# The second block's output projection from F32 matmuls to high and low parts, with the splitting put into the tail of the mixer

## Chip, cores and metric

One core of a Trainium2 chip runs the whole kernel. The metric is the device time of one execution in microseconds, the median over runs. The kernel before takes 2604.84 us, median of three runs (2599.87 to 2604.89). The profiled execution is another one.

Names of the engines: PE is TensorE, PEld its weight loads, DVE is VectorE, ACT is ScalarE, SP issues the DMAs of the weights, POOL those of the modulation rows.

## The reference, cut to what matters

The program chains two transformer stacks over 256 latent tokens (and, in the second stack, 256 context tokens), model width 1024. The change is in the last layer of the second stack, layer 1, where only the latent tokens go on:

```
q, k, v = split(h @ w_in)                      # 16 heads of 64, 4 key/value heads
o_lat   = window_gqa(q, k, v, ...)             # softmax(q k + window mask, with sink) v
o_lat   = o_lat @ w_out                        # [256, 1024] @ [1024, 1024]   <- the change
x       = x + m_lat[5] * o_lat
x       = x + 0.5 * m_lat[8] * swiglu(modulate(rms_norm(x), ...), ffn_in, ffn_out)
return rms_norm(x, final_gain)
```

Everything is float32. A product `x @ w` is made in this kernel in one of two ways. Either as it stands, a matmul of type F32. Or on parts: `hi` is the operand rounded by a copy to the type fp32r (float32 "round"), `lo` is the operand less `hi`, also as fp32r, and the product is `w_hi x_hi + w_hi x_lo + w_lo x_hi`, three matmuls of type fp32r into the same bank of PSUM.

## The kernel before

The activations lie feature-major, `[128 partitions, 8 chunks (KC), tokens]`. Five engines run programs of their own, in order, and wait for each other by semaphores. The function `schedule` names the stages; each engine supplies its own version of each stage, and `barrier` between stages lets no engine go on before PE, ACT and DVE have drained.

Weights come as tiles of 1 MB (1024 rows by 256 columns, `TILE`) in the order of `weight_order`, into a ring of three slots (`RING`). SP asks for tile n once tile n-3 has been released (`tile_used`). A tile has two halves (m = 0, 1) of 128 output features.

PSUM has eight banks. All engines take them in the same order (`turns`); PE takes the bank after next only when the user of eight turns ago has freed it (`take_bank`, `bank_free`).

**The mixer of layer 1**, `blend(1)`, with `blend_order(1)`: the values, then ten halves of q and k (`half` 0 to 9), each a product on parts of 24 fp32r matmuls of 512 columns. For each half ACT copies the high part of the weights (`split_high`, line 1795) and DVE subtracts the low part (`split_low`, line 2306). Behind each half comes a `rope` step (PE line 1139, DVE lines 2444 to 2447). Beside them runs the attention, 16 pairs of units, chunk `j` of the output `ph4["o"]` made by pairs 2j and 2j+1. The steps, called "pair" i, are software-pipelined (`attention_pairs`), and within step i the engines do, each in this order:

- PE: the scores of pair i (line 1198), the outputs of pair i-3 (line 1214), the transposes of pair i-2 (line 1226)
- ACT: evicts the outputs of pair i-3 into `o` (line 1907), copies the two transposed p of pair i-2 to `pT` (line 1912), two exps of pair i (line 1918)
- DVE: for both units of pair i adds the mask and takes the maximum (lines 2511, 2512), then rescales pair i-1 (lines 2518, 2523)

Halves and steps interleave as half 9, rope 8, steps 10 and 11, rope 9, then steps 12 to 18 with no half left. Steps 16 to 18 have no scores any more. This stretch from step 10 on is called the tail of the mixer below. Then follow the barrier and the projection.

**The projection of layer 1**, `project("w_out_2o", 1, SEQ)`: 8 output chunks, for each 8 F32 matmuls (line 983) of 256 columns, read from the ring tile. The profile shows two records of each F32 matmul. Between tiles PE waits until the last product of the tile is complete (`take_tile`, line 901). For each chunk DVE adds the gated product to x (`gated_add`, line 2417), ACT squares it (line 1783), and PE sums the squares for the coming norm with F32 matmuls (`sum_squares`, line 938), two chunks at a time, in between.

**The projection of layer 0**, `project_parts`, is on parts already: it splits at its start the eight chunks of `o` and two weight halves, and one further half per chunk (lines 992, 1666, 2373). It follows the recurrence, and runs 512 tokens.

Of the kernel before, what the change touches and what calls it, by code (L numbers as in the profile page):

```python
# [32 lines left out]
P = 128  # L33
# [156 lines left out]
def schedule(s):  # L190
# [16 lines left out]
    s["project_parts"](TOK)  # L207
# [11 lines left out]
    s["project"]("w_out_2o", 1, SEQ)  # L219
# [74 lines left out]

def blend_order(layer):
# [11 lines left out]
    for at, item in enumerate(main + [("none", 0)]):  # L307
        yield item
        for what, later in places:
            for i, begun in enumerate(evicted):  # L310
                if begun + later == at:
                    yield what, i
        for i, place in enumerate(pairs):
            if place == at:
                yield "pair", i
        if layer == 0 and at == 19:
            yield "lora", 0

# [8 lines left out]
def weight_order():  # L327
# [7 lines left out]
    def project(name, layer, tok):  # L335
        for j in range(4):
            order.append((name, 0, j))

    def project_parts(tok):
        for j in range(4):  # L340
            order.append(("w_out_2e", 0, j))
# [24 lines left out]
    schedule(dict(blend=blend, project=project, project_parts=project_parts, mixer=mixer, leave=leave, ffn=ffn, **{n: quiet for n in names}))  # L366
# [39 lines left out]
def out_halves(order):  # L406

    at = order.index(("w_out_2e", 0, 0))
    return [Half("out", at + c // 2, c % 2, 0, KC, c) for c in range(KC)]
# [25 lines left out]
def build(nc, ins, out):  # L435
    order = weight_order()
    with ExitStack() as ctx:
# [70 lines left out]
        with ExitStack() as stack:  # L508
# [10 lines left out]
            for ph in (ph2, ph3):  # L519
# [4 lines left out]
                            "x_hi": parts_of_x, "x_lo": parts_of_x, "w_hi": parts_of_w, "w_lo": parts_of_w})  # L524
# [8 lines left out]
        parts_out = out_halves(order)  # L533
# [16 lines left out]


# [327 lines left out]
        def _(pe):  # L879
# [89 lines left out]
            def project(name, layer, tok):  # L969
                o = ph4["o"] if layer else ph2["o"]  # L970
                for c in range(KC):
                    m = c % 2
                    if m == 0:
                        w = take_tile()
                    bank, full = take_bank()
                    product = turns.n - 1
                    if m == 1 and c > 1:
                        sum_squares(c - 3, tok)
                        sum_squares(c - 2, tok)
                    for kc in range(KC):  # L980
                        if c == KC - 1 and kc == KC - 2:
                            sum_squares(KC - 2, tok)
                        mm = pe.matmul(bank[:, 0:tok], w[:, kc * COLS + m * P:kc * COLS + (m + 1) * P],  # L983
                                       o[:, kc, 0:tok], start=kc == 0, stop=kc == KC - 1)
                        if kc == 0:
                            first(mm)
                    mm.then_inc(full, 1)
                    if m == 1:
                        release_tile(product)
                sum_squares(KC - 1, tok)  # L990

            def project_parts(tok):

                b_w, b_o = tally("w_split", KC), tally("o_split", KC)
                for c, h in enumerate(parts_out):
# [5 lines left out]
                    high, low = mixed_half(0)(c)  # L1001
# [3 lines left out]
                    for kc in range(KC):  # L1005
# [4 lines left out]
                        hi, lo = ph2["x_hi"][:, kc, 0:tok], ph2["x_lo"][:, kc, 0:tok]  # L1010
# [603 lines left out]
            def store():  # L1614
# [4 lines left out]
                start=start, norm=norm_and_count, blend=blend, project=project, project_parts=project_parts, mixer=mixer, leave=leave,  # L1619
# [4 lines left out]
        def _(act):  # L1624
# [31 lines left out]
            def project(name, layer, tok):  # L1656
                for c in range(KC):
                    if c == 4:
                        sums.append(turns.next())
                    if c == KC - 2:  # L1660
                        exp_and_ln()
                    b, use = turns.next()
                    act.wait_ge(bank_free[b], use + 1)
                    square(c, tok)

            def project_parts(tok):
                used = tally("w_used", KC - 1)
                act.dma_start(c_silu[:], ins["c"]).then_inc(sem("c_in"), 16)
                split_high(parts_out, 0, used, mixed_half(0), 0)
                for kc in range(KC):  # L1670
                    nc.scalar.activation(ph2["x_hi"][:, kc, 0:tok], ph2["o"][:, kc, 0:tok], ACT.Copy).then_inc(sem("o_hi_ready"), 1)
                split_high(parts_out, 1, used, mixed_half(0), 0)
                came = []
                for c in range(KC):
                    if 2 <= c + 1 < KC:
                        split_high(parts_out, c + 1, used, mixed_half(0), 0)
                    if c == 4:
                        sums.append(turns.next())
                    if c == 5:
# [13 lines left out]
            def blend(layer):  # L1693
# [38 lines left out]
                for what, i in blend_order(layer):  # L1732
# [56 lines left out]
            def split_high(halves, n, used, place=split_half, private=EARLY):  # L1789
# [3 lines left out]
                if n >= SPLITS + private:  # L1793
                    act.wait_ge(sem("w_used"), used + n - SPLITS + 1)
# [100 lines left out]
            def attention_pairs(us):  # L1895
# [5 lines left out]
                def step(i):  # L1901
                    taken = [turns.next() for _ in range(2)] if i < n else []
                    if i >= lag + 1:
# [3 lines left out]
                        nc.scalar.activation(u.dst, bank[:, 0:k * P].rearrange("p (k t) -> p k t", k=k), ACT.Copy).then_inc(free, 1)  # L1907
                    if lag <= i < n + lag:
# [285 lines left out]
            def norm_counted(kind, which, tok, summed=None):  # L2194
# [5 lines left out]
                start=start, norm=norm_counted, blend=blend, project=project, project_parts=project_parts, mixer=mixer, leave=leave,  # L2200
# [4 lines left out]
        def _(dve):  # L2205
# [160 lines left out]
            def project(name, layer, tok):  # L2366
                for c in range(KC):
                    if c == 4:
# [3 lines left out]

            def project_parts(tok):
                b_o = tally("o_hi_ready", KC)
                split_low(parts_out, 0, mixed_half(0))
                for kc in range(KC):
                    dve.wait_ge(sem("o_hi_ready"), b_o + kc + 1)
                    V.tensor_tensor(ph2["x_lo"][:, kc, 0:tok], ph2["o"][:, kc, 0:tok], ph2["x_hi"][:, kc, 0:tok].bitcast(F32),
                                    ALU.subtract).then_inc(sem("o_split"), 1)
                split_low(parts_out, 1, mixed_half(0))  # L2380
                for c in range(KC):
                    if 2 <= c + 1 < KC:
                        split_low(parts_out, c + 1, mixed_half(0))
                    if c == 4:
                        sums.append(turns.next())
                    bank, free = full_bank()
                    gated_add(bank, free, 0, 5, c, tok)

            def blend(layer):
# [6 lines left out]
                for what, i in blend_order(layer):  # L2396
# [293 lines left out]
            def recurrence():  # L2690
# [186 lines left out]
                start=start, norm=norm, blend=blend, project=project, project_parts=project_parts, mixer=mixer, leave=leave,  # L2877
# [114 lines left out]
```

## Time and profile before

| what | us |
|---|---|
| median of three runs | 2604.84 |
| lowest, highest | 2599.87, 2604.89 |
| the profiled execution | 2601.52 |
| its span | 2599.7 |
| PE busy in the span | 2442.0 (94%) |
| DVE busy | 1454.3 (56%) |
| ACT busy | 875.5 (34%) |
| the mixer's tail, from step 10's scores to the barrier | 2325.0 to 2350.8 |
| the projection of layer 1 | 2350.9 to 2383.6 |

Times within the execution are counted from the start of the span. A row of the timeline gives start, length, engine, line, operation, output<-input, shapes and, in brackets, how long the engine stood idle ahead of it and who ended the wait. The end of a matmul is modelled, so consecutive matmuls overlap in their lengths; their distance is read from the starts.

### The profile page before, as it was taken

To read this page: it belongs to the slowest core of one execution; us is meant where nothing else is said; L and a number is where in the kernel's file an instruction comes from. 1 tells how busy PE (TensorE), PEld (TensorE's weight loads), DVE (VectorE), ACT (ScalarE), POOL (GpSimd) and SP (SyncE) were. 2 spreads that over 40 slices of the span, in tenths; PEclk is the share of its full clock that TensorE was granted. 3 is DMA by queue.
4 is the path that set the end of the run, shared out by engine and by line. 5 is a ranking of instruction groups with operands and counts; after the bars stand their busy time and mean duration, and the time that the engine had idled before them with its cause. 6 is when DMAs were issued, how large, how long until landed. Compare 5 with 4: busy or idle time off the path is not lost.

```text
span 2599.7 us, 41895 instructions
## 1 busy us (share of the span) xinstructions
PE 2442.0 (94%) x17718; PEld 1989.0 (77%) x17718; DVE 1454.3 (56%) x2326; ACT 875.5 (34%) x1491; POOL 76.5 (3%) x148
## 2 busy tenths in 40 slices
PE   8999999999999999678887999999999999999998
PEld 6687778688887767567875788877688877777997
DVE  5555565655554578666544555545655554563553
ACT  2341132422222435532224422222422222454543
POOL 0000000000000000000000000000000000000000
PEclk9999999999999999798989999999999999999999
DMA  8236526344434310000003344444344433202553
GB/s 299 99 115 218 185 98 210 138 146 135 140 138 146 132 65 33 1 3 4 4 3 130 107 144 139 137 140 145 129 138 145 136 144 125 93 33 84 190 180 130
DMA packets 55913, 310.91 MB, mean 120 GB/s; under 512 B 5936, under 2 KB 9392, under 8 KB 28080
## 3 DMA queue, kind: packets, MB, share of 16 engines
q1 hardware_dynamic: 32944, 224.75, 24.3%
q0 software_dynamic: 20736, 75.51, 8.8%
q10 hardware_dynamic: 2048, 7.98, 0.8%
q8 instruction: 141, 2.31, 0.4%
q14 instruction: 44, 0.36, 0.0%
HBM read 307.16 MB, written 1.05 MB: 119 GB/s over the span
## 4 chain that ended last, share of the span: by engine, by line
PEld 42%; PE 30%; issue 12%; DVE 10%; ACT 5%; PEldq 0%; DMA 0%; DVEq 0%; SPq 0%; ACTq 0%
PEld bank L1410 14%; PEld bank L1403 13%; PEld bank L1406 12%; PE bank L1252 5%; PE bank L1461 4%; PE bank L1249 2%; PE bank L1311 2%; PE bank L1327 2%; PE bank L1067 1%; PE bank L1074 1%; PE bank L1070 1%; PE bank L1139 1%; PE bank L983 1%; ACT hn L1832 1%; DVE ms L2293 1%
## 5 line engine op out<-in xcount | busy, mean ns | idle before, releaser
L2306 DVE TENSOR_TENSOR w_lo<-ring,w_hi 128x1024 fp32r<-128x1024 f32 (+1 forms) x195 | 232.5, 1192 | 441.1 <-ACT w_hi L1795 441.1
L1403 PE MATMUL bank<-ffn_x_hi,w_hi 128*128 128x512 f32 x984 | 388.7, 395 | 0.0
L1406 PE MATMUL bank<-ffn_x_lo,w_hi 128*128 128x512 f32 x984 | 388.7, 395 | 0.0
L1410 PE MATMUL bank<-ffn_x_hi,w_lo 128*128 128x512 f32 x984 | 388.7, 395 | 0.0
L1795 ACT ACTIVATE w_hi<-ring 128x1024 fp32r<-128x1024 f32 (+1 forms) x195 | 200.5, 1028 | 282.0 <-PE bank L1406 271.0
L2235 DVE SCALAR_TENSOR_TENSOR ms<-mod_rows,c_silu 128x1024 f32<-128x1024 f32 x200 | 244.0, 1220 | 1.3
L1403 PEld LDWEIGHTS bank<-ffn_x_hi,w_hi 128*128 128x128 f32 x984 | 184.4, 187 | 45.2
L1406 PEld LDWEIGHTS bank<-ffn_x_lo,w_hi 128*128 128x128 f32 x984 | 184.4, 187 | 45.2
L1410 PEld LDWEIGHTS bank<-ffn_x_hi,w_lo 128*128 128x128 f32 x984 | 184.4, 187 | 45.0
L1403 PE MATMUL bank<-ffn_h_hi,w_hi 128*128 128x512 f32 x528 | 213.4, 404 | 0.0
L1410 PE MATMUL bank<-ffn_h_hi,w_lo 128*128 128x512 f32 x528 | 208.6, 395 | 0.0
L1406 PE MATMUL bank<-ffn_h_lo,w_hi 128*128 128x512 f32 x528 | 208.5, 395 | 0.0
L1252 PE MATMUL bank<-hn,ring 128*128 128x256 f32 x768 | 174.5, 381 | 3.3 <-PE bank L1252 3.0
L1252 PEld LDWEIGHTS bank<-hn,ring 128*128 128x128 f32 x768 | 143.1, 190 | 30.1 <-issue 12.5
L2052 ACT ACTIVATE ffn_h_hi<-rs 128x512 fp32r<-128x512 f32 (+1 forms) x88 | 51.0, 580 | 318.7 <-DVE rs L2676 318.7
L875 POOL DMA_DIRECT2D mod_rows<-in_mod_stream x144 | 76.3, 530 | 2091.7 <-DVEq L2238 1567.2
L2046 ACT ACTIVATE sq<-bank 128x512 f32<-128x512 f32 (+1 forms) x88 | 47.8, 543 | 225.3 <-PE bank L1410 224.8
L2235 DVE SCALAR_TENSOR_TENSOR one_products<-mod_rows,c_silu 128x1024 f32<-128x1024 f32 x88 | 107.6, 1223 | 27.1 <-DMA mod_rows<-in_mod_stream 22.3
L2316 DVE TENSOR_TENSOR ffn_h_lo<-ring,ffn_h_hi 128x1024 fp32r<-128x1024 f32 (+1 forms) x68 | 80.5, 1192 | 73.7 <-ACT ffn_h_hi L1803 73.7
L1406 PEld LDWEIGHTS bank<-ffn_h_lo,w_hi 128*128 128x128 f32 x528 | 99.0, 187 | 26.6 <-issue 2.9
L1403 PEld LDWEIGHTS bank<-ffn_h_hi,w_hi 128*128 128x128 f32 x528 | 99.0, 188 | 26.5 <-issue 2.9
L1410 PEld LDWEIGHTS bank<-ffn_h_hi,w_lo 128*128 128x128 f32 x528 | 99.0, 187 | 24.2
(456 smaller groups left out, 4580.6 us busy)
## 6 DMA issues: line engine op xcount, KB each, us to landing
ring<-in_stream SPq DMA_DIRECT2D x211, 1024.0 KB, 4.8
mod_rows<-in_mod_stream POOLq DMA_DIRECT2D x144, 512.0 KB, 3.8
one_const<-in_one ACTq DMA_DIRECT2D x1, 1665.0 KB, 14.5
mix_const<-in_two ACTq DMA_DIRECT2D x1, 1440.0 KB, 6.6
win_const<-in_win ACTq DMA_DIRECT2D x1, 1216.0 KB, 5.2
x<-in_x SPq DMA_DIRECT2D x4, 256.0 KB, 4.7
c_silu<-in_c SPq DMA_DIRECT2D x1, 1024.0 KB, 10.3
x<-in_x SPq DMA_DIRECT2D x1, 1024.0 KB, 26.8
```

The lines of the kernel that those rows point to most:

```text
L875: pool.dma_start(mod_rows[:, n % 2, :], ins["mod_stream"][n]).then_inc(sem(f"mod_rows_in{n % 2}"), 16)
L1249: mm = pe.matmul(bank[:, 0:COLS], hn[:, kc, m * P:(m + 1) * P], w[:, kc * COLS:(kc + 1) * COLS], start=kc == 0, stop=kc == KC - 1)
L1252: mm = pe.matmul(bank[:, 0:SEQ], w[:, kc * COLS + m * P:kc * COLS + (m + 1) * P], hn[:, kc, 0:SEQ], start=kc == 0, stop=kc == KC - 1)
L1311: mm = pe.matmul(bank[:, 0:SEQ], w[:, kc * COLS + m * P:kc * COLS + (m + 1) * P], ph1["o"][:, kc, :], start=kc == 0, stop=kc == KC - 1)
L1403: mm = pe.matmul(bank[:, 0:tok], w_high, hi, start=k == 0, stop=False)
L1406: mm = pe.matmul(bank[:, 0:tok], w_high, lo, start=False, stop=False)
L1410: mm = pe.matmul(bank[:, 0:tok], w_low, hi, start=False, stop=last)
L1461: mm = pe.matmul(part(bank[r, col]), lhs[r, col], part(rhs[r, col]), start=True, stop=True)
L1795: nc.scalar.activation(place(n)[0][:, 0:h.nk, :], raw_half(h), ACT.Copy).then_inc(sem("w_hi_ready"), 1)
L2235: link(V.scalar_tensor_tensor(products[:].rearrange("p a b -> p (a b)"), mod_rows[:, part // 2, :], 1.0, c_silu[:, part % 2, :], ALU.mult, ...
L2306: V.tensor_tensor(low[:, 0:h.nk, :], raw_half(h), high[:, 0:h.nk, :].bitcast(F32), ALU.subtract).then_inc(sem("w_split"), 1)
L2316: V.tensor_tensor(low[:, 0:h.nk // 2], raw_last(h), high[:, 0:h.nk // 2].bitcast(F32), ALU.subtract).then_inc(sem("w_split"), 1)
```

## The change

The projection of layer 1 becomes `project_parts(1, SEQ)`. `project` is gone. The parts of `o` and the first four weight halves are made in the tail of the mixer instead of in the projection; for this the parts of the weights get four slots in layer 1 instead of two (half n goes to slot (n+2) mod 4, so that halves 0 and 1 don't use the slots that the mixer's own halves have). A place list says after which pair step each is made:

```diff
+OUT_SPLIT_AFTER = 10, 11, 13, 14
+OUT_PARTS_AFTER = 13, 13, 14, 14, 15, 16, 18, 18
...
             if place == at:
                 yield "pair", i
+                if layer:
+                    for n in range(4):
+                        if OUT_SPLIT_AFTER[n] == i:
+                            yield "out_weight", n
+                    for c in range(KC):
+                        if OUT_PARTS_AFTER[c] == i:
+                            yield "out_parts", c
...
-    s["project"]("w_out_2o", 1, SEQ)
+    s["project_parts"](1, SEQ)
...
+        def out_half(layer):
+            if layer == 0:
+                return mixed_half(0)
+            return lambda n: (ph4["w_hi"][:, (n + SPLITS) % 4], ph4["w_lo"][:, (n + SPLITS) % 4])
```

PE (the F32 matmuls of line 983 are replaced by the three of `project_parts`, now for both layers):

```diff
-            def project_parts(tok):
+            def project_parts(layer, tok):
...
-                high, low = mixed_half(0)(c)
+                high, low = out_half(layer)(c)
...
-                        hi, lo = ph2["x_hi"][:, kc, 0:tok], ph2["x_lo"][:, kc, 0:tok]
+                        hi, lo = mixed[layer]["x_hi"][:, kc, 0:tok], mixed[layer]["x_lo"][:, kc, 0:tok]
```

ACT (in the blend loop "out_weight" calls `out_weight(1, i)`; "out_parts" waits for the evictions of pairs 2i and 2i+1 and calls `out_high`):

```diff
+            def out_weight(layer, n):
+                if n == 0:
+                    out_used[0] = tally("w_used", KC - 1)
+                split_high(parts_out[layer], n, out_used[0], out_half(layer), 0, OUT_SLOTS[layer])
+
+            def out_high(layer, kc, tok):
+                o = (ph4 if layer else ph2)["o"]
+                nc.scalar.activation(mixed[layer]["x_hi"][:, kc, 0:tok], o[:, kc, 0:tok], ACT.Copy).then_inc(sem("o_hi_ready"), 1)
...
                 for c in range(KC):
+                    if OUT_SLOTS[layer] <= c + OUT_SLOTS[layer] - 1 < KC:
+                        out_weight(layer, c + OUT_SLOTS[layer] - 1)
...
+                    elif what == "out_weight":
+                        out_weight(1, i)
+                    elif what == "out_parts":
+                        act.wait_ge(sem("came_out"), 2 * i + 2)
+                        out_high(1, i, SEQ)
...
                         nc.scalar.activation(u.dst, bank[:, 0:k * P].rearrange("p (k t) -> p k t", k=k), ACT.Copy).then_inc(free, 1)
+                        if u.bufs is ph4:
+                            wait_read(free)
+                            act.nop().then_inc(sem("came_out"), 1)
```

DVE:

```diff
+            def out_low(layer, kc, tok):
+                if kc == 0:
+                    out_base[0] = tally("o_hi_ready", KC)
+                dve.wait_ge(sem("o_hi_ready"), out_base[0] + kc + 1)
+                o, to = (ph4 if layer else ph2)["o"], mixed[layer]
+                V.tensor_tensor(to["x_lo"][:, kc, 0:tok], o[:, kc, 0:tok], to["x_hi"][:, kc, 0:tok].bitcast(F32),
+                                ALU.subtract).then_inc(sem("o_split"), 1)
...
                 for c in range(KC):
+                    if OUT_SLOTS[layer] <= c + OUT_SLOTS[layer] - 1 < KC:
+                        split_low(parts_out[layer], c + OUT_SLOTS[layer] - 1, out_half(layer))
...
+                    elif what == "out_weight":
+                        split_low(parts_out[1], i, out_half(1))
+                    elif what == "out_parts":
+                        out_low(1, i, SEQ)
```

Halves 4 to 7 of layer 1 are split within the projection, three chunks ahead. In `project_parts` PE counts a tile as released when its second half begins (it has been split by then), and the ring slot is free from the first matmul of that half on. Layer 0 does what it did.

## Rows read from the trace of the kernel before

**Rows 1.** Busy time by stretch (columns: stretch, length, busy and count by engine, clock, DMA)

```profile
2326.00:2338.00 12.00, 11.89 (x114) 9.15 (x114) 11.26 (x29) 7.56 (x23) 0.00 (x0) 1.00 0.00 1
...
2344.80:2350.90 6.10, 4.25 (x49) 3.25 (x49) 0.94 (x4) 3.48 (x11) 0.00 (x0) 1.00 0.00 0
...
2350.90:2383.60 32.70, 31.61 (x142) 26.63 (x142) 3.43 (x8) 2.92 (x7) 0.00 (x0) 1.00 0.29 97
```

**Rows 2.** Chain of waits, tail of the mixer and projection (columns: start, length, what)

```profile
2340.27 0.81 PE bank L1226 x6
...
2341.07 1.38 PE bank L1198 x12
...
2347.20 0.88 PE bank L1214 x12
...
2348.59 0.88 ACT win_pT L1912 x2
...
2349.61 0.89 PE bank L1214 x12
...
2350.88 7.19 PE bank L983 x32
...
2358.07 0.38 issue
...
2362.14 0.86 PE bank L938 x4
...
2363.01 3.47 PE bank L983 x16
```

**Rows 3.** Timeline of PE, last FFN, the first and the last of 25 matmuls

```profile
2399.79 0.28 PE L1403 MATMUL bank<-ffn_x_hi,ffn_h_hi 128*128 128x256 f32 x1
...
2402.67 0.28 PE L1403 MATMUL bank<-ffn_x_hi,ffn_h_hi 128*128 128x256 f32 x1
```

**Rows 4.** Timeline of DVE, tail of the mixer

```profile
2329.86 0.29 DVE L2511 TENSOR_TENSOR bank<-bank,win_const 128x128 f32<-128x128 f32 x1
...
2332.32 0.68 DVE L2444 TENSOR_TENSOR tmp<-bank,win_const 128x512 f32<-128x512 f32 x1
...
2334.60 0.30 DVE L2511 TENSOR_TENSOR bank<-bank,win_const 128x128 f32<-128x128 f32 x1
...
2336.21 0.16 DVE L2518 RECIPROCAL stats<-stats 128x2 f32<-128x2 f32 x1
...
2337.06 0.29 DVE L2511 TENSOR_TENSOR bank<-bank,win_const 128x128 f32<-128x128 f32 x1
```

**Rows 5.** Timeline of ACT and PE, tail of the mixer

```profile
2335.53 0.58 ACT L1918 ACTIVATE win_p<-bank,stats 128x386 f32<-128x386 f32 x1
...
2337.20 0.87 PE L1226 MATMUL bank<-base,win_p 128*128 128x128 f32 x6
...
2350.52 0.28 ACT L1907 ACTIVATE win_o<-bank 128x128 f32<-128x128 f32 x1 [1.06 <-PE bank L1214]
```

**Rows 6.** Timeline, splits in the mixer (L1795, L2306) and in the last norm

```profile
2307.42 0.59 ACT L1918 ACTIVATE win_p<-bank,stats 128x386 f32<-128x386 f32 x1
...
2307.98 1.07 ACT L1795 ACTIVATE win_w_hi<-ring 128x1024 fp32r<-128x1024 f32 x1
...
2309.09 1.22 DVE L2306 TENSOR_TENSOR win_w_lo<-ring,win_w_hi 128x1024 fp32r<-128x1024 f32 x1 [1.34 <-ACT win_w_hi L1795]
...
2389.63 0.42 ACT L1837 ACTIVATE ffn_x_hi<-hn 128x256 fp32r<-128x256 f32 x1
...
2390.08 0.42 DVE L2334 TENSOR_TENSOR ffn_x_lo<-hn,ffn_x_hi 128x256 fp32r<-128x256 f32 x1 [0.29 <-ACT ffn_x_hi L1837]
...
2390.42 0.42 DVE L2339 TENSOR_TENSOR hn<-x,rstd 128x256 f32<-128x256 f32 x1
```

**Rows 7.** Busy time by stretch, recurrence of layer 0

```profile
1104.00:1112.00 8.00, 3.90 (x104) 2.75 (x103) 7.12 (x14) 0.60 (x1) 0.00 (x0) 0.92 0.01 2
...
1112.00:1116.00 4.00, 3.89 (x103) 3.52 (x103) 3.41 (x9) 1.19 (x2) 0.00 (x0) 0.73 0.02 4
```

More of the change, by code:

```diff
@@ L206, in schedule @@
     s["barrier"]()
-    s["project_parts"](TOK)
+    s["project_parts"](0, TOK)
     s["barrier"]()
@@ L333, in blend @@
             order.append((name, 0, j))
-    def project(name, layer, tok):
+    def project_parts(layer, tok):
         for j in range(4):
-            order.append((name, 0, j))
-    def project_parts(tok):
-        for j in range(4):
-            order.append(("w_out_2e", 0, j))
+            order.append((OUT_NAMES[layer], 0, j))
     def mixer(layer):
@@ L532, in build @@
         parts_of = [blend_halves(order, layer) for layer in range(2)]
-        parts_out = out_halves(order)
+        parts_out = [out_halves(order, layer) for layer in range(2)]
         def split_half(n):
@@ L967, in norm_and_count, with project_parts @@
                 tally("normed", KC)
[L969 to L992, printed above, removed]
+            def project_parts(layer, tok):
                 b_w, b_o = tally("w_split", KC), tally("o_split", KC)
-                for c, h in enumerate(parts_out):
+                for c, h in enumerate(parts_out[layer]):
                     pe.wait_ge(sem("w_split"), b_w + c + 1)
@@ L1654, in start, with project_parts @@
                 nc.scalar.activation(c_silu[:], c_silu[:], ACT.Silu).then_inc(sem("c_silu_ready"), 1)
-            def project(name, layer, tok):
+            def out_weight(layer, n):
[5 more added lines that the diff above has]
+                nc.scalar.activation(mixed[layer]["x_hi"][:, kc, 0:tok], o[:, kc, 0:tok], ACT.Copy).then_inc(sem("o_hi_ready"), 1)
+            out_used = [0]
+            def project_parts(layer, tok):
+                if layer == 0:
+                    act.dma_start(c_silu[:], ins["c"]).then_inc(sem("c_in"), 16)
+                    out_weight(0, 0)
+                    for kc in range(KC):
+                        out_high(0, kc, tok)
+                    out_weight(0, 1)
+                came = []
                 for c in range(KC):
+                    if OUT_SLOTS[layer] <= c + OUT_SLOTS[layer] - 1 < KC:
+                        out_weight(layer, c + OUT_SLOTS[layer] - 1)
                     if c == 4:
                         sums.append(turns.next())
[L1660 to L1679, printed above, removed]
+                    if c == 5 and layer == 0:
                         other_table()
@@ L2371, in project @@
                     gated_add(bank, free, layer, 5, c, tok)
[L2373 to L2387, printed above, removed]
             def blend(layer):
@@ L2876, in _ @@
             schedule(dict(
-                start=start, norm=norm, blend=blend, project=project, project_parts=project_parts, mixer=mixer, leave=leave,
+                start=start, norm=norm, blend=blend, project_parts=project_parts, mixer=mixer, leave=leave,
                 barrier=barrier, ffn=ffn, recurrence=recurrence, store=quiet))
```

29 lines of the change are left out of this document (19 added, 10 removed).

## Prediction

> **What bounds the kernel now.** I read the stages around the change first. In the busy time by stretch [rows 1], from 2326 to 2338 us TensorE (PE) is busy 11.89 of 12.00 us, but VectorE (DVE) is busy 11.26: there is hardly any free DVE time in the tail of the mixer. From 2344.8 to 2350.9 PE is busy only 4.25 of 6.10. In the projection, 2350.9 to 2383.6, PE is busy 31.61 of 32.70 us and DVE 3.43, at full clock.
>
> The chain of waits [rows 2] then shows what the end is made of. Each of the last three mixer steps is a circle PE, ScalarE (ACT), PE: outputs at 2347.20, transposes, two copies of pT on ACT at 2348.59, outputs again at 2349.61 (2.41 us a circle, three of them). The projection is PE throughout: 16 records take 3.47 us, 0.217 each. The 64 F32 matmuls of 256 columns are 128 records, two each, so one costs 0.434 us. At the end of a tile PE stands still for some 0.4 us.
>
> **The projection, after.** The 64 F32 matmuls go, and with them the wait for a tile's last product ahead of each next tile. Now: 128 x 0.217 = 27.8 us; seven of the eight sums of squares lie inside, two of them (four records) taking 0.86, so 7 x 0.43 = 3.0; the stretch is 32.7 us long, of which 0.4 is the way from the last product to its use, which stays. The rest, 32.3 - 27.8 - 3.0 = 1.5, is the three tile ends, 0.5 us each: a pause as that of 0.38 us, and the pipe filling again. New: 8 x 8 x 3 = 192 matmuls of fp32r with 256 columns. The second block's last FFN has just this form; there the 25th starts 2.88 us after the first [rows 3], 2.88 / 24 = 0.120 each. 192 x 0.120 = 23.0, and with 3.0 for the sums of squares 26.0 us, without tile stops, since PE now releases a tile when its second half begins. Saving 32.3 - 26.0 = **6.2 us** (rounded as worked with more digits). Halves 4 to 7 are split inside the projection, three halves ahead. In all DVE is busy 3.43 us there now [rows 1] and gets 4 x 1.22 more, ACT 2.92 and 4 x 1.07 more [rows 6], 8.3 and 7.2 us of 26. A half takes PE 2.9 us, and one is split some 3 us after its slot comes free, while over 8 remain. So they are hidden. The fourth tile is requested when the second half begins, 2.9 us in, rather than 7.3, and the first FFN tiles come earlier too; nothing there waited for a load. I bound the saving by 5.2 us (a gap of 0.2 us at each of five waits) and 8.4 (a matmul of fp32r at a quarter of the 0.434 of F32, 0.1085 each).
>
> Here the Trainium skill (TensorE: Matmul & The Clock Gate, Back-to-back issue gap) would give more: isolated back-to-back matmuls start every N/2.4 + 2.5 ns, 109 ns at 256 columns. By it the 192 take 21.0 us and the saving is 8.3. The rows of this kernel say 120 ns, and I go by them.
>
> **The tail of the mixer, after.** Four weight halves and eight output chunks are split there: ACT copies the high part, DVE subtracts. DVE executes in order, so a subtraction that waits for ACT holds up the next step's mask adds, maxima and rescaling, and PE behind them. DVE's own times [rows 4]: a full step (two masked maxima and a rescaling) goes from 2334.60 to 2337.06, 2.46 us, of which the rescaling is 0.85 (2336.21 to 2337.06), the maxima 1.61; a rope step 2332.32 to 2334.60, 2.28 us. From ACT [rows 5]: an exp starts 0.93 us after its mask add (2334.60 to 2335.53). Of the splits [rows 6]: ACT goes on 0.56 after the start of a step's second exp (2307.42 to 2307.98); DVE can subtract 1.11 after ACT starts a weight's high part (2307.98 to 2309.09) and is through in 1.14 (1.22 long; the next instruction starts 0.08 before an end, as 2390.08 and 0.42 against 2390.42 show). An output chunk is as large as the FFN's 128x256 ones: DVE may start 0.45 after ACT (2389.63 to 2390.08) and is through in 0.34 to 0.36.
>
> How long DVE waits for a weight: the second mask add starts 0.81 + 0.85 = 1.66 us before DVE gets to the split; the high part lands 0.93 + 0.56 + 1.11 = 2.60 after it. So 0.94 us of standing still. After step 13 ACT is itself late with the exps (it had to copy a pT that waited for the late rescaling), and I take 1.2 us.
>
> The chain on DVE, counted from 2329.86, where step 10 ends in the old trace:
> after step 10: 0.94 + 1.14, to 2331.9. Step 11: 2.46, to 2334.4. After it 0.94 + 1.14, to 2336.5. Rope: 2.28, to 2338.8. Steps 12 and 13: 4.92, to 2343.7. After 13, one weight half and two chunks: 1.2 + 1.14 + 0.7, to 2346.8. Step 14: 2.46, to 2349.2. After it 0.94 + 1.14 + 0.7, to 2352.0. The maxima of step 15: 1.61, to 2353.7; there the rescaling for the 15th pair (unit pair 14) begins.
> PE transposes it 0.99 us after the rescaling starts (2336.21 to 2337.20 in the old trace) [rows 4, 5], at 2354.6. A circle is 2.41 us from outputs to outputs, 0.81 of it before the transposes [rows 2], so from transposes to outputs 1.6, and the last outputs start at 2358.7, where they started at 2349.61 before: 9.1 us later. Chunks 4 and 5 sit beside these circles (0.34 us on ACT and on DVE, in idle time).
>
> At the end something new lies before the barrier. The last eviction starts 0.91 after the outputs (2349.61 to 2350.52) [rows 2, 5], at 2359.6. ACT then waits for its own write (some 0.4 us from its start), and makes the high parts of chunks 6 and 7 (0.34, then 0.45 until DVE may take the second), DVE subtracts (0.42): 2361.2. Before, PE started the projection at 2350.88, 0.08 after the last eviction ended; now at 2361.3. The tail is **10.4 us** longer. The nops behind the 16 evictions cost some 0.2 us of ACT each, and I cost them at nothing: in a circle the eviction starts 0.91 after the outputs, at 2348.11, and the copies of pT at 2348.59 [rows 2], since PE transposes first. Without that cover it would be 0.2 a circle.
>
> Bounds of this term. From below: if no handover stood still (ACT's parts ready whenever DVE comes), the chain is shorter by 4 x 0.94 + 0.3 = 4.1: +6.3. Lower still, +1.3 (from 2359.6 + 0.28, where the eviction ends, to 2361.2), if DVE's 6 us of new work fell in idle time altogether; rows 1 speak against it (0.74 us idle in 12). Nothing is taken out of this stretch, so there is no gain in it. From above: +13, with 0.2 us more in each of a dozen handovers. I take 10.4, since each link comes from a row.
>
> **Sum.** 10.4 - 6.2 = +4.2 us. The profiled execution took 2601.5 us with a span of 2599.7, 1.8 around it; by its own time the sum is 2605.7. The median of the three runs is 3.3 us above the profiled one (two runs at 2604.9, one at 2599.9); I forecast on the median: **2609.0 us**. About 0.2%, 5.2 us, is what a measurement of this kernel can tell from no change, and +4.2 is inside it.
>
> **The rivals.**
> Clock. From 2338 to 2361 PE would have two score groups at 1.38, six outputs and five transposes at 0.81 [rows 2], 11.7 us of 23, 50%. In the recurrence, 8 us with PE busy 3.90 ended with the clock at 0.92, and the next 4 us went at 0.73 though PE was busy 3.89 of them [rows 7]. If that comes here, the projection begins at the 1.2 GHz level. Those 12 us lost 8 x 0.08 + 4 x 0.27 = 1.7 us; a start of 4 us wholly at the low level costs 2 to 4. Sum +6 to +8: 2612, slower. Against it: 4.25 of 6.10 us busy at the end of the tail left the clock at 1.00 [rows 1]. The Trainium skill (TensorE: Matmul & The Clock Gate, The HAM clock gate) says that an idle PE falls to half rate; the rows show one after 8 us in which PE worked for 3.90. It decides if the clock has fallen when the projection begins. Chance 0.25.
>
> Cover. The splits fall in idle time of ACT and DVE, only the last chunks show: 1.3 - 6.2 = -4.9, 2599.9, at the edge of faster, and -7.1 with the upper saving. For it: over the whole span DVE is busy 56%. Against it: rows 1 and 4, DVE is not idle where the splits are put. Chance 0.12, two thirds of it faster by over 0.2%.
>
> Matmuls. One of fp32r costs a quarter of one of F32, 0.1085: the gain is 8.4, the sum +2.0, 2606.8. Rows 3 speak against it. The gap that the Trainium skill gives comes to the same. Chance 0.08, no change.
>
> No standing still. ACT's parts are always there first: +6.3 - 6.2 = 0: 2605. Chance 0.05, no change.
>
> **Chances.** The forecast's own case has 0.50, from +2.5 to +6.5 (2607 to 2611.5); a third of it lies beyond 5.2. Faster 0.08, all from cover. Slower: 0.17 of the forecast and 0.22 of the clock, 0.39. Same: 0.33 + 0.03 + 0.04 + 0.08 + 0.05 = 0.53. The range 2602 to 2615 takes in the clock's upper price and the case without standing still, with two or three us for which level of the runs the median hits; beyond it are most of cover and a clock that stays low for long.
>
> **What would show it.** Projection: 192 fp32r matmuls 0.120 apart, about 26 us from the first to the last, no pause at tile ends. Tail: DVE waits of about 0.9 us for the high parts of the weights after steps 10, 11, 13 and 14, PE waiting for the rescaled p and for banks from step 12 on, and the first matmul of the projection about 10 us later against the start of step 10. The chunks 6 and 7 between the last eviction and the barrier: 1.5 us. Wrong if PE reaches the barrier less than 6 us late (cover), if the matmuls are not 0.120 apart, or if the granted clock falls below 1.00 in the first 5 us of the projection.

## The result, and the profile after

In its own comparison the changed kernel took 2608.18 us (median of 20 runs, 2605.01 to 2614.75) against 2602.14 for the kernel before (20 runs, 2599.87 to 2606.64). The ratio is 1.0026, with a 95% interval of 1.0020 to 1.0032: slower by 5.2 to 8.3 us. The prediction said 2609.0 and a range of 2602 to 2615. It held "within 0.2%" (0.53) for likelier than "slower" (0.39), and the kernel is slower by 0.26%.

The 20 times of the changed kernel lie in two groups, eleven from 2605.0 to 2608.3 us and nine from 2611.2 to 2614.8, with nothing between. The mean granted clock over an execution is 0.973 to 0.976 in the first group and 0.970 to 0.973 in the second. The kernel before goes from 2599.9 to 2606.6 without such a gap. The traced execution of the changed kernel is the shortest of its 20.

The profiled run took 2605.01 us (span 2603.2; before 2601.52 and 2599.7). I cut both traces at three points: the start of the score matmuls of step 10, the first matmul of the projection, and the start of the last gated add. The stretch between the first two is "the tail" below, that between the last two "the projection".

| | tail | projection | last add to the end |
|---|---|---|---|
| before | 2325.00 to 2350.88: 25.88 | to 2383.56: 32.68 | 216.14 |
| after | 2323.67 to 2360.70: 37.03 | to 2387.02: 26.32 | 216.18 |
| difference | **+11.15** | **-6.36** | +0.04 |

The two stretches make +4.8 us. The span grew by 3.5 only, because the tail began 1.3 us earlier; in the kernels below that have the same work ahead of it, that start lay between 2322.6 and 2332.2, so it is scatter between executions.

Busy time of the changed kernel by stretch (columns as in rows 1), cut about where PE's work or the granted clock changes:

```profile
2323.70:2335.70 12.00, 11.40 (x105) 8.62 (x104) 9.85 (x20) 7.62 (x19) 0.00 (x0) 1.00 0.00 0
2335.70:2340.00 4.30, 0.88 (x13) 0.64 (x13) 3.98 (x11) 1.51 (x5) 0.00 (x0) 0.76 0.01 2
2340.00:2348.40 8.40, 8.40 (x45) 6.67 (x45) 6.42 (x17) 5.78 (x15) 0.00 (x0) 0.51 0.01 3
2348.40:2360.70 12.30, 6.49 (x72) 5.03 (x70) 6.83 (x18) 8.00 (x23) 0.00 (x0) 1.00 0.00 0
2360.70:2387.00 26.30, 26.28 (x206) 25.71 (x206) 8.29 (x11) 6.71 (x11) 0.00 (x0) 1.00 0.43 147
```

The last line is the new projection: PE busy 26.28 of 26.30 us at full clock, where it was 31.61 of 32.70 [rows 1]. In the second line PE is nearly idle while DVE is busy 3.98 of 4.30: there the tail is DVE's. In the third PE is busy all the time, at the 1.2 GHz level (0.51), and DVE 6.42 of 8.40.

DVE's timeline in the first part of the tail, with the instructions behind a weight's subtraction (L2309):

```profile
2327.87 0.75 DVE L2531 TENSOR_SCALAR win_p<-win_p,stats 128x384 f32<-128x384 f32 x2
2329.45 1.23 DVE L2309 TENSOR_TENSOR win_w_lo<-ring,win_w_hi 128x1024 fp32r<-128x1024 f32 x1 [0.83 <-ACT win_w_hi L1795]
2330.59 0.29 DVE L2519 TENSOR_TENSOR bank<-bank,win_const 128x128 f32<-128x128 f32 x1
...
2333.97 1.22 DVE L2309 TENSOR_TENSOR win_w_lo<-ring,win_w_hi 128x1024 fp32r<-128x1024 f32 x1 [0.83 <-ACT win_w_hi L1795]
...
2337.39 0.30 DVE L2519 TENSOR_TENSOR bank<-bank,win_const 128x128 f32<-128x128 f32 x1
...
2341.65 0.75 DVE L2531 TENSOR_SCALAR win_p<-win_p,stats 128x384 f32<-128x384 f32 x2
2344.17 1.23 DVE L2309 TENSOR_TENSOR win_w_lo<-ring,win_w_hi 128x1024 fp32r<-128x1024 f32 x1 [1.77 <-ACT win_w_hi L1795]
...
2349.65 1.23 DVE L2309 TENSOR_TENSOR win_w_lo<-ring,win_w_hi 128x1024 fp32r<-128x1024 f32 x1 [1.12 <-ACT win_w_hi L1795]
```

The brackets show what a subtraction costs apart from its own 1.14 us: DVE stands still for 0.83, 0.83, 1.77 and 1.12 us until ACT's high part is there, and the mask add of the next step (L2519) waits behind it. PE's timeline shows who pays:

```profile
2336.57 0.88 PE L1208 MATMUL bank<-win_pT,win_v 128*64 128x128 f32 x12 [1.12 <-DVE win_q L2453]
2340.00 1.54 PE L1220 MATMUL bank<-base,win_p 128*128 128x128 f32 x6 [2.55 <-DVE win_p L2531]
2341.47 1.65 PE L1192 MATMUL bank<-win_q 64*128 64x192 f32 x8
...
2354.06 0.88 PE L1220 MATMUL bank<-base,win_p 128*128 128x128 f32 x6 [1.65 <-DVE win_p L2531]
```

PE pauses 1.12 and 2.55 us for DVE, and the transposes at 2340.00 take 1.54 us where they take 0.88 at full clock (2354.06). The granted clock, 1.00 until the first of these pauses was over, fell some 0.5 us into the second, at about 2338. From 2340.00 on the chain of waits (what ended last, step by step) goes through PE at the low level for 7.03 us, before it comes back to ACT and DVE:

```profile
2339.19 0.76 DVE win_p L2531 x2
...
2340.00 1.54 PE bank L1220 x6
2341.54 2.52 PE bank L1192 x12
2344.06 1.48 PE bank L1208 x12
2345.54 1.49 PE bank L1220 x6
2347.05 0.49 ACT win_pT L1915
```

At full clock such groups take 0.81, 1.38, 0.88 and 0.87 us [rows 2, 5], so that an estimate from these rows puts the clock's share of the tail at 3.1 us at the most. DVE would not have been ready for all of it: the waits of 1.77 and 1.12 us exceed the earlier 0.83 by 1.2 us together, and that is the likelier share, also an estimate. The chain of waits at the end of the tail, through the new work ahead of the barrier:

```profile
2358.08 0.89 PE bank L1208 x12
2358.99 0.29 ACT win_o L1907
...
2359.39 0.42 ACT win_x_hi L1657
2359.84 0.43 DVE win_x_lo L2374
2360.27 0.39 DVEq L2431
...
2360.70 0.19 PEld bank L1005
```

From the last eviction to the first matmul 1.71 us pass, 0.36 before [rows 2, 5]. In the projection PE's timeline gives the price of the new matmul:

```profile
2362.72 0.28 PE L1008 MATMUL bank<-win_x_lo,win_w_hi 128*128 128x256 f32 x1
2362.84 0.28 PE L1012 MATMUL bank<-win_x_hi,win_w_lo 128*128 128x256 f32 x1
2362.96 0.28 PE L1005 MATMUL bank<-win_x_hi,win_w_hi 128*128 128x256 f32 x1
2363.08 0.28 PE L1008 MATMUL bank<-win_x_lo,win_w_hi 128*128 128x256 f32 x1
```

One starts every 0.120 us, as in rows 3. The Trainium skill (TensorE: Matmul & The Clock Gate, Back-to-back issue gap) gives 109 ns for isolated matmuls, and says that in a stream with weight loads both set the distance; the trace decides for 120 here.

### The profile page after: what moved, and what is told of

Its sections match the earlier page's. It is cut to its first block, busy times and chain, and to the rows that moved or that the text cites. A ratio compares the mean times of both kernels' runs of the same rounds, so it can differ in the third digit from the quotient of the medians.

```text
span 2603.2 us, 42074 instructions
## 1 busy us (share of the span) xinstructions
PE 2440.3 (94%) x17782; PEld 1991.8 (77%) x17782; DVE 1467.1 (56%) x2342; ACT 886.1 (34%) x1507; POOL 76.5 (3%) x148
## 4 chain that ended last, share of the span: by engine, by line
PEld 42%; PE 29%; issue 12%; DVE 10%; ACT 5%; PEldq 0%; DVEq 0%; DMA 0%; ACTq 0%; SPq 0%
PEld bank L1404 14%; PEld bank L1397 13%; PEld bank L1400 12%; PE bank L1246 5%; PE bank L1455 3%; PE bank L1243 2%; PE bank L1305 2%; PE bank L1321 2%; PE bank L1061 1%; PE bank L1068 1%; PE bank L1064 1%; PE bank L1133 1%; PEld bank L1005 1%; PEld bank L1012 1%; PEld bank L1008 1%
## 5 line engine op out<-in xcount | busy, mean ns | idle before, releaser
L2309 DVE TENSOR_TENSOR w_lo<-ring,w_hi 128x1024 fp32r<-128x1024 f32 (+1 forms) x195 | 232.5, 1192 | 441.0 <-ACT w_hi L1795 441.0
L1795 ACT ACTIVATE w_hi<-ring 128x1024 fp32r<-128x1024 f32 (+1 forms) x195 | 200.5, 1028 | 282.0 <-PE bank L1400 271.0
L1246 PEld LDWEIGHTS bank<-hn,ring 128*128 128x128 f32 x768 | 143.9, 191 | 30.5 <-issue 12.5
```

What stands on the lines that cost most here:

```text
L1246: mm = pe.matmul(bank[:, 0:SEQ], w[:, kc * COLS + m * P:kc * COLS + (m + 1) * P], hn[:, kc, 0:SEQ], start=kc == 0, stop=kc == KC - 1)
L1795: nc.scalar.activation(place(n)[0][:, 0:h.nk, :], raw_half(h), ACT.Copy).then_inc(sem("w_hi_ready"), 1)
L2309: V.tensor_tensor(low[:, 0:h.nk, :], raw_half(h), high[:, 0:h.nk, :].bitcast(F32), ALU.subtract).then_inc(sem("w_split"), 1)
```

## The experiments

Two theories went in. **A**: DVE takes its work in order; 6 us of new work and the waits for ACT lie on the chain of the tail. **B**: the low clock, or simply the number of splits and handovers, makes the tail long. These are two causes, and a run that speaks against the number does not by that speak against the clock. Every experiment is the changed kernel with the edit shown, in five rounds beside the kernel before. The stretches are those of the first table; the clock is the granted one, by stretch. They come from one traced execution of each kernel, the ratio from all of them. The edits are shown in outline.

| kernel | tail | projection | ratio to before | 95% interval |
|---|---|---|---|---|
| before | 25.88 | 32.68 | | |
| after | 37.03 | 26.32 | 1.0026 | 1.0020 to 1.0032 |
| e1_f32_projection | 37.12 | 30.96 | 1.0045 | 1.0031 to 1.0059 |
| e2_no_splits_in_tail | 25.98 | 26.31 | 0.9981 | 0.9972 to 0.9990 |
| e3_weights_late | 31.07 | 28.52 | 1.0009 | 0.9999 to 1.0019 |
| e4_into_the_gaps | 27.13 | 26.31 | 0.9985 | 0.9976 to 0.9993 |
| e5_low_one_step_later | 31.09 | 26.32 | 1.0003 | 0.9994 to 1.0012 |
| e6_filled_pauses | 39.04 | 27.81 | 1.0038 | 1.0025 to 1.0050 |
| e7_weights_early_only | 28.44 | 26.30 | 0.9986 | 0.9978 to 0.9995 |
| e8_outputs_late_only | 37.93 | 26.31 | 1.0029 | 1.0018 to 1.0040 |
| e9_fills_while_it_waits | 38.49 | 27.64 | 1.0029 | 1.0019 to 1.0038 |

**The tail alone: e1_f32_projection.** The splits stay, the projection goes back to F32, but keeps the new order of waits (by split half, without `take_tile`).

```
-  pe.matmul(bank, high[:, kc, :], hi, ...)   # and two more: high*lo, low*hi
+  pe.matmul(bank, w[:, kc * COLS + h.m * P:...], ph4["o"][:, kc, 0:tok], ...)
```

> The tail of the mixer is that of the changed kernel, all splits included, but the projection is made by the 64 F32 matmuls on the raw weights and outputs (the parts are made and not used; PE no longer waits for a tile's last product, the release comes with the next tile's first matmul). Theory A (the splits cost the tail 11 us because DVE executes in order: 6 us of new work and four waits for ACT; the projection gives 6 back): 11.2 us more than before in the tail, 0 to 1.5 us less in the projection for the missing tile ends, so 9.7 to 11.2 us slower than before, 2612 to 2613.5 on a median of 2602. Theory B (the tail costs little, the clock that falls in and after it costs the most, and F32 matmuls after it suffer as well): 4 to 8 us slower. First projection matmul some 37 us after the scores of step 10 by either.

Measured: 2613.28 us (five executions) against 2601.14. The time is in theory A's range, but that range was counted from 2602; the difference, 12.1 us by the medians and 11.7 by the ratio, lies above its 9.7 to 11.2, and the two stretches give 9.5. The tail is as long as after's (37.12). The projection takes 30.96 us, with PE busy 30.92 of 31.00 and no pause between tiles. So the 6.36 us that the projection gained come apart: 4.64 (30.96 to 26.32) are the cheaper matmuls, 1.72 the end of `take_tile`'s three pauses [rows 2], which F32 matmuls get as well.

**The projection alone: e2_no_splits_in_tail.**

```
-  if OUT_SPLIT_AFTER[n] == i:        yield "out_weight", n
-  if OUT_PARTS_AFTER[c] == i:        yield "out_parts", c
+  (neither)
```

PE no longer waits for these parts and takes the first four weight halves and the parts of `o` from whatever lies in the buffers; the kernel leaves out their making, and its result is not the reference's.

> The changed projection alone: 192 fp32r matmuls, halves 4 to 7 split in it, but nothing split in the tail (the first four halves and the outputs are taken from what lies in the buffers, so the result is not the reference's; the evictions' wait and nop stay). Theory A: the tail is as before (25.9 us from step 10's scores to the first matmul, no fall of the clock), the projection 26.3 instead of 32.7 us: 6.4 us faster than before, 2595.7. If the nops behind the evictions cost something, it shows here as a tail longer than 25.9. Rival (the gain of the projection is smaller, 4 or less, since its splits of halves 4 to 7 or the fp32r matmuls cost): 2598 or more.

Measured: 2596.53 us (before 2601.14). The tail is 25.98, that of before. All of the 11 us belongs to the splits in the tail, and the projection's gain is real: 6.37 us in its stretch. Of these the total shows 4.9 by the ratio, with an interval of 2.6 to 7.3.

**Where the weights are split: e3_weights_late.**

```
-OUT_SPLIT_AFTER = 10, 11, 13, 14
+OUT_SPLIT_AFTER = 15, 16, 17, 18
```

> The four weight halves are split after steps 15, 16, 17, 18 instead of 10, 11, 13, 14; the output chunks stay where they are. Theory A: DVE has idle time there (3 to 4 us before the barrier in the kernel before), three of the four waits no longer stand ahead of a rescaling: the tail is 5 us shorter than in the changed kernel, 2603, about 1 us slower than before, and the last half shows ahead of the barrier with 2 us. Theory B (the number of splits counts, not their place, ACT and DVE being full anyway): as the changed kernel, 2607 to 2608.

Measured: 2604.5 us against 2601.14, with an interval that takes in no change. The tail falls to 31.07 us, since after step 15 DVE has little other work, as theory A has it; but here the projection is 2.2 us longer than in all kernels that begin it at full clock. Busy time by stretch of this kernel:

```profile
2349.00:2351.00 2.00, 0.88 (x12) 0.66 (x12) 1.06 (x3) 1.76 (x5) 0.00 (x0) 1.00 0.00 0
2351.00:2353.00 2.00, 0.00 (x0) 0.00 (x0) 1.65 (x2) 1.62 (x3) 0.00 (x0) 0.81 0.00 0
2353.00:2354.00 1.00, 0.00 (x0) 0.00 (x0) 0.94 (x3) 0.00 (x0) 0.00 (x0) 0.50 0.00 0
2354.00:2355.00 1.00, 0.96 (x4) 0.96 (x5) 0.00 (x0) 0.00 (x0) 0.00 (x0) 0.50 0.00 0
...
2356.00:2358.00 2.00, 2.00 (x11) 2.00 (x11) 0.00 (x0) 0.00 (x0) 0.00 (x0) 0.50 0.04 8
2358.00:2360.00 2.00, 2.00 (x15) 2.00 (x14) 0.48 (x1) 0.26 (x1) 0.00 (x0) 0.73 0.00 0
2360.00:2365.00 5.00, 5.00 (x44) 5.00 (x44) 2.94 (x3) 2.48 (x4) 0.00 (x0) 1.00 0.60 210
```

PE stands still for 3.5 us ahead of the barrier (the last outputs end at 2350.5, the projection begins at 2354.04), the clock falls to the 1.2 GHz level in that pause, 1.7 us after its start, and PE, busy without a gap, gets full speed back only at about 2359. This is the rival "clock" of the prediction, in another kernel: a start at the low level cost 2.2 us here.

**Into the gaps: e4_into_the_gaps.** Three weight halves go ahead of the part in which DVE is full, the fourth and most chunks behind it.

```
-OUT_SPLIT_AFTER = 10, 11, 13, 14
-OUT_PARTS_AFTER = 13, 13, 14, 14, 15, 16, 18, 18
+OUT_SPLIT_AFTER = 9, 9, 9, 16
+OUT_PARTS_AFTER = 13, 15, 16, 17, 17, 17, 17, 18
```

> Weight halves 0, 1, 2 after step 9 (DVE stands idle for 5.0 us there while PE makes half 9 of the mixer, ACT for 3.8), half 3 after step 16, output chunks after 13, 15, 16, 17, 17, 17, 17, 18. Theory A: the three halves vanish in the idle time, the rest costs 1.5 us ahead of the barrier (last chunk) and next to nothing in the steps, no long pause of PE, so no fall of the clock: tail +1.5, projection -6.4, 5 us faster than before, 2597. Theory B (place does not matter): 2607 to 2608.

Measured: 2596.72 us, ratio 0.9985. It beats both kernels, the one before by 0.15%, with an interval of 0.07 to 0.24%. All splits are there and the tail is only 1.25 us longer than before. DVE's timeline of this kernel has all four weights:

```profile
2319.76 3.50 DVE L2309 TENSOR_TENSOR win_w_lo<-ring,win_w_hi 128x1024 fp32r<-128x1024 f32 x3 [1.33 <-ACT win_w_hi L1795]
...
2346.56 1.23 DVE L2309 TENSOR_TENSOR win_w_lo<-ring,win_w_hi 128x1024 fp32r<-128x1024 f32 x1 [0.81 <-ACT win_w_hi L1795]
```

Three subtractions in one run wait once for ACT, before the tail begins; and the last outputs start 24.79 us after the scores of step 10, where it was 24.61 before and 34.41 after.

**The order on DVE: e5_low_one_step_later.** ACT makes the high parts after the same steps; DVE subtracts after the score work of the next pair step.

```
 elif what == "pair":
     scores(i)
+    for later in waiting:
+        later()
+    waiting.clear()
 elif what == "out_weight":
-    split_low(parts_out[1], i, out_half(1))
+    waiting.append(lambda i=i: split_low(parts_out[1], i, out_half(1)))
```

(the same for the chunks)

> As the changed kernel, with the same 20 new DVE and ACT operations after the same steps on ACT, but DVE executes each subtraction only after the score work of the next step of the same kind, so ACT's high part is long there when DVE comes to it. Theory A (the tail is set by DVE's order: 6 us of new DVE work and 4.5 us in which DVE stands still for ACT): the four waits for w_hi (0.83, 0.83, 1.77, 1.12) go, the tail is 31 to 32.5 us instead of 37.0, the span some 5 us shorter than after's and the median about 2602.5 to 2603.5. Theory B (the number of splits in the tail or the clock it brings counts, not the order): nothing moves, 37 us and 2608.

Measured: 2601.72 us against 2600.79, which can't be told from no change (0.9994 to 1.0012). Theory A, counted from 2602, had 2602.5 to 2603.5. The tail is 31.09, in its range. The same instructions, as many handovers, and 5.94 us less. The weight's subtraction after step 11 in DVE's timeline of this kernel:

```profile
2329.40 0.75 DVE L2537 TENSOR_SCALAR win_p<-win_p,stats 128x384 f32<-128x384 f32 x2
2330.07 1.22 DVE L2309 TENSOR_TENSOR win_w_lo<-ring,win_w_hi 128x1024 fp32r<-128x1024 f32 x1
2331.20 0.68 DVE L2458 TENSOR_TENSOR tmp<-bank,win_const 128x512 f32<-128x512 f32 x1
```

No bracket: DVE goes from the rescaling to the subtraction to the rope without standing still. And the clock stays up in the tail:

```profile
2322.70:2334.70 12.00, 12.00 (x117) 9.29 (x116) 11.14 (x25) 7.79 (x20) 0.00 (x0) 1.00 0.00 0
2334.70:2353.80 19.10, 11.38 (x118) 8.77 (x114) 15.37 (x39) 14.68 (x42) 0.00 (x0) 1.00 0.01 2
```

This experiment decides against the number of splits and handovers, and for the order on DVE. It does not separate the order from the clock: the waits and the fall of the clock went together, in the traced execution, and the brackets account for 4.55 of the 5.94 us. What remains of the tail's excess is 5.2 us. Of it 1.4 stand between the last eviction and the first matmul, as after the change; the rest is part of DVE's own new work, 4 x 1.14 and 8 x 0.35, or 7.4 in all, of which some falls in idle time.

**Which splits cost: e7_weights_early_only and e8_outputs_late_only.** The edit of e4, one line each.

```
e7: +OUT_SPLIT_AFTER = 9, 9, 9, 16        (OUT_PARTS_AFTER as in the change)
e8: +OUT_PARTS_AFTER = 13, 15, 16, 17, 17, 17, 17, 18   (OUT_SPLIT_AFTER as in the change)
```

> OUT_SPLIT_AFTER is 9, 9, 9, 16 (three weight halves ahead of the part in which DVE has no gap, the fourth behind it); the output chunks stay where the change puts them. Theory A (weights cost most: 4 x 1.14 of DVE and four waits for ACT; the chunks are short): the tail is 28 to 29.5 us, of 37.0 after and 27.1 with the chunks moved as well, and the median about 2598. Theory B (every handover counts the same, eight chunks against four halves): two thirds of the ten us stay, tail 33 to 34, median 2604.

> The converse: the weights stay where the change puts them, OUT_PARTS_AFTER is 13, 15, 16, 17, 17, 17, 17, 18. Theory A: the chunks after steps 13 and 14 leave the chain of DVE (4 x 0.35 = 1.4 us), and one stays at the end: the tail is 35.5 to 36, the median 2606.5 to 2607. Theory B (every handover counts the same): seven us of the eleven go, tail 30, median 2601.

Measured: e7 2598.75 us (before 2600.79), tail 28.44, as theory A has it; e8 2607.64 us (before 2600.79), tail 37.93, which neither theory has. Moving the weights takes away 8.6 us of the 11.15. Moving the chunks as well takes 1.3 more (e7 to e4), but without the weights it takes nothing. In e8 the clock is at the low level for longer than after:

```profile
2340.00:2345.00 5.00, 2.45 (x14) 2.07 (x14) 4.79 (x14) 2.82 (x8) 0.00 (x0) 0.71 0.01 3
2345.00:2350.00 5.00, 5.00 (x30) 3.89 (x28) 3.16 (x8) 3.17 (x9) 0.00 (x0) 0.50 0.01 3
2350.00:2355.00 5.00, 5.00 (x30) 3.91 (x28) 3.45 (x9) 2.99 (x8) 0.00 (x0) 0.50 0.00 0
2355.00:2360.00 5.00, 3.66 (x29) 2.89 (x30) 2.50 (x9) 3.49 (x10) 0.00 (x0) 0.58 0.00 0
```

There DVE waits 1.77, 1.45, 1.15, 1.28 and 1.98 us in place of the change's 1.77, 1.12, 0.19, 0.37 and 3.56. And the chain of waits of e8 runs through PE alone for 12.5 us:

```profile
2342.60 1.54 PE bank L1220 x6
2344.15 2.52 PE bank L1192 x12
...
2353.62 1.49 PE bank L1220 x6
```

So the low clock was on the path in e8, ahead of DVE's order. That it cost the 2 us over theory A's 36 fits these rows; no run gives the price apart.

**Holding the clock up: e6_filled_pauses and e9_fills_while_it_waits.** Matmuls that compute nothing used are put into PE's pauses.

```
 bank, full = take_bank()
+if n == 16 and i == 13:      # e6: one ahead of the outputs, three ahead of the transposes
+    pe.matmul(bank[:, 0:3 * P], ident, base[:, 0:3 * P], start=True, stop=True)
+fill = {13: 2, 15: 2, 16: 2}.get(i, 0)     # e9: ahead of the transposes; two ahead of the outputs of 16
```

> As the changed kernel, but in PE's two long pauses of the step in which the clock fell (1.12 and 2.55 us) it runs four matmuls of the identity with 384 columns of F32 into banks that the next products overwrite. They compute nothing that is used, and PE waits for the rescaled p after them as before. Theory A: the granted clock stays at 1.00 through the tail (it was 0.79, 0.50, 0.68 in 2335 to 2350), but the tail is set by DVE, and becomes only 0.7 us shorter (36.3 of 37.0): 2607 to 2608. Theory B (the clock's fall makes the tail long): the six groups that ran at the low level get back some 0.7 us each, 4 us in all, and the median falls to 2604.

> As the changed kernel, with eight matmuls of the identity (384 columns of F32, some 0.7 us each, computing nothing that is used) only where PE has its bank and waits for DVE's rescaled p or ACT's pT: two ahead of the transposes of steps 13, 15 and 16, and two ahead of the outputs of step 16. The 1.12 us pause ahead of the outputs of step 13 stays empty, since there PE waits for the bank itself. Theory A (DVE's order sets the tail, the clock only adds): the granted clock is higher than after's 0.79, 0.50, 0.68, the tail is 36.3 to 37, the projection 26.3, the median 2607 to 2608. Theory B (the low clock makes the tail long): the tail falls to 33, the median to 2604. If the fall only comes later, as in the kernel with filled pauses, the tail is over 37 again and the clock can't be held by these fills.

Both theories missed in e6, and in e9 what came is the third case of its expectation, a fall that only comes elsewhere: 2610.42 us for e6 (five executions, against 2600.79) and 2612.6 for e9 (against 2604.6; the traced execution is the longest of its eleven), with tails of 39.04 and 38.49 us. The clock fell all the same, at 2350.4 in e6 and ahead of the first fill in e9, and it was at the low level at the start of the projection too (27.81 and 27.64). PE's timeline of e6, and then busy time by stretch of the same kernel:

```profile
2337.41 0.91 PE L1201 MATMUL bank<-base 128*128 128x384 f32 x2 [1.12 <-DVE win_q L2460]
...
2339.88 2.20 PE L1223 MATMUL bank<-base 128*128 128x384 f32 x6 [0.75 <-ACT win_p L1928]
2341.92 0.82 PE L1227 MATMUL bank<-base,win_p 128*128 128x128 f32 x6
```

```profile
2345.00:2350.00 5.00, 3.16 (x32) 2.47 (x31) 4.25 (x10) 3.76 (x11) 0.00 (x0) 1.00 0.00 0
2350.00:2355.00 5.00, 2.45 (x18) 1.68 (x17) 4.25 (x10) 3.76 (x11) 0.00 (x0) 0.54 0.00 0
```

The pause of 1.12 us is a wait for the bank itself, so the fill came behind it, not in it: the outputs start 7.84 us after the rope's matmuls, 7.01 after the change; the transposes 11.51 after them instead of 10.44. The fills were on the path. In e9 the one known fault was avoided, but the first fill (four records, 2.93 us) already ran at the low level and held up the transposes by 1.8 us (12.22 after the rope). So these two runs don't give the clock's price in the changed kernel. They show only that these fills lengthened the tail, by 2.0 and 1.5 us.

## Why the prediction was right, and where it was off

The mechanism held in the traced execution: +4.2 forecast, +4.8 in the two stretches, with both terms near their sizes. That 2609.0 came within 0.8 us of the median, 2608.2, is partly luck. The forecast was 2604.84 and 4.2; the kernel before had its median at 2602.14 in 20 runs, 2.7 lower, and the difference of the medians was 6.0, 1.8 higher, and the two errors cancel. Point by point:

- **Projection, -6.2 predicted, -6.36 measured.** 192 matmuls 0.120 apart, no pauses; e1 splits it as the text did: 4.8 and 1.5 predicted, 4.64 and 1.72 measured. The splits of halves 4 to 7 stay hidden (PE busy 26.28 of 26.30).
- **The tail, +10.4 predicted, +11.15 measured.** The text's chain on DVE holds link by link up to step 13. Its times less 1.33, the earlier start of the tail (2325.00 to 2323.67), against the rows: end of the first subtraction 2330.6 and 2330.6; of the second 2335.2 and 2335.1; mask add of step 12 2337.5 and 2337.39; end of step 13 2342.4 and 2342.4 (2341.65 with 0.75). Then it parts: the next step 14 was due at 2345.5 and came at 2346.0.
- **The mis-sized term** is the wait for ACT after step 13: taken as 1.2 us, measured 1.77; the next, taken as 0.94, measured 1.12. Together 0.75 us, which is all of the excess. ACT's copies of pT and the exps behind them came late because PE's transposes ran at the 1.2 GHz level (1.54 us for 0.88), after pauses that the text had not worked out for PE. So the account by DVE alone holds up to step 13 only: from 2340.00 to 2347.03 the chain of waits is PE's. The link from the clock to the wait is read from the order of the rows; no run separated it.
- **Ahead of the barrier**: 1.7 us from the last eviction to the first matmul predicted, 1.71 measured.
- **Rival clock.** It was put at the wrong place. The clock fell, but in the tail (0.76, then 0.51), was back by 2348.4, and was 1.00 in the projection, so that the 2 to 4 us there were not paid. The text worked out PE's busy share of the new tail, but not its single pauses, and looked for the price in the projection alone. The fall came inside a pause of 2.55 us (after) and inside one of 3.5 us (e3), in e6 0.5 us behind one. The Trainium skill (TensorE: Matmul & The Clock Gate, The HAM clock gate) has an idle PE fall to half rate, and the trace of the changed kernel agrees in so far: 1.00 before, 0.50 at the end of the pause.
- **Rival cover** (the splits fall in idle time) fell for this placement, and is true of another: e4 has it whole, -5.1 us in the two stretches where the rival said -4.9. The prediction took the placement as given, and rightly, but the same rows (DVE busy 0.94 of 6.10 us at the end of the tail [rows 1]) already said where the work would have been free.
- **Rival no standing still**: it priced the four waits at 4.1 us. e5 took away 5.94: the waits (4.55 by the brackets), and with them the fall of the clock; which part of the other 1.4 us is the clock's was not measured.
- **Rival matmuls** fell: 0.120, not 0.1085.
- **Same or slower.** +4.2 against a bound of 5.2 us was rightly seen as close; the median came 6.0 higher, on the other side, and the ratio's interval (5.2 to 8.3) has the forecast's +4.2 outside. The stretches of the one profiled run of each kernel give +4.8, 0.4 us below that interval. Most kernels here show this (e1 +9.5 by the trace and +11.7 by the ratio, e2 -6.3 and -4.9, e4 -5.1 and -3.9, e5 -1.2 and +0.8, e8 +5.7 and +7.5), some don't (e7 -3.8 and -3.6, e9 +7.6 and +7.5). Part of it is which execution was traced: the shortest of 20 for the changed kernel, while the longer ones have a lower mean clock (0.970 to 0.973). So other executions did lose more to the clock, and the size of the forecast's miss against the median stays open to that extent; in which stage they lost it, no trace shows.

## What to carry to other kernels

An instruction that waits for another engine, put into an in-order stream that has no slack, cost its wait as well as its own time here: queue the first half of a handover one step ahead of the second (e5: 5.9 us for the same work), or batch the work where that engine idles (e4: 9.9 us). Moving work from a stage with a full PE into one that another engine bounds must be priced by the second stage. And a pause that such work makes on PE can have a second price, the clock, paid where PE is next busy: 2.2 us in the projection of e3, and in the tail itself after the change, where it is estimated only. A traced execution is one of many: look where its time lies among the others before a few us are read from it.

## What the runs showed of the hardware

- The granted clock fell within short pauses or right behind one: after the change from 1.00 (2335 to 2337) to 0.50 (2339 to 2340), some 0.5 us into a pause of 2.55 us that followed one of 1.12, and it was back at 1.00 after 8.2 us in which PE was busy without a gap. In e3 it fell 1.7 us into a pause of 3.5 us and was back after some 5 us of unbroken matmuls. In e5, with PE busy 11.38 of 19.10 us and a longest pause of 2.16, it stayed at 1.00; in e6 it fell 0.5 us after a pause of 1.65 had ended. So the length of a single pause does not tell these cases apart.
- A matmul of fp32r with 256 columns starts every 0.120 us, three of them 0.36, one in F32 0.434: the high and low parts save 17% of PE's time here, and need two operations per operand on other engines.
- An edit that took work off DVE's chain did not shorten the tail while PE was at the low level: e8 moved three chunks out of the steps in which DVE has no slack, the clock stayed at 0.50 for longer (2342 to 2359), and the tail became 0.9 us longer.
